# Building the token table of a mixture-of-experts layer: scatters to DRAM against matmuls of 0/1 rows

## The reference, cut to what matters

```python
expert_id = g_idx * EXPERTS_PER_GROUP + e_local        # two experts for each token, of 32
dest = pstart[e_sorted] + (jnp.arange(A) - start[e_sorted])   # a slot for each (token, choice)
x_disp = jnp.zeros((P, D), h.dtype).at[dest].set(h[t_sorted]) # blocks of rows, one expert each
def expert_block(args):
    xb, e = args
    return (jax.nn.silu(xb @ w_gate[e]) * (xb @ w_up[e])) @ w_down[e]
contrib = (w_sorted[:, None] * y_disp[dest].astype(jnp.float32))
out = jnp.zeros((T, D), jnp.float32).at[t_sorted].add(contrib)
```

## Time and profile before

| what | us |
|---|---|
| median of three runs | 3354.77 |
| lowest, highest | 3348.31, 3357.60 |
| span of the profiled execution | 3367.8 |
| PE busy in it | 2546.5 (76%) |
| DVE busy in it | 1126.7 (33%) |
| ACT busy in it | 943.4 (28%) |
| POOL busy in it | 375.3 (11%) |

### The profile page before, as it was taken

The page is one execution under the profiler, slowest core; times in us unless marked ns, Lnnn a source line. Parts: engine busy times, 40 slices in busy tenths (PEclk is TensorE's granted clock), DMA queues, the critical chain, the costliest instruction groups (busy, mean ns, idle before and its releaser), DMA issues. The chain is left out here.

```text
span 3367.8 us, 50960 instructions
## 1 busy us (share of the span) xinstructions
PE 2546.5 (76%) x17895; PEld 1960.9 (58%) x17896; DVE 1126.7 (33%) x2432; ACT 943.4 (28%) x1720; POOL 375.3 (11%) x716
## 2 busy tenths in 40 slices
PE   5974798387778759699897388884969898648773
PEld 4964698154445438576676266653847676536562
DVE  4446334210001025447443211115634653311113
ACT  2233322121112122246322033322234532113221
POOL 0000000111111110000000223221000000122222
PEclk9987899698889879799998588886979998768896
DMA  3201221699999953122121789994122123299995
GB/s 115 77 1 51 76 88 51 222 369 374 374 369 369 374 189 120 32 63 63 48 55 63 238 248 302 313 295 136 51 56 62 45 58 89 82 293 303 307 326 173
DMA packets 416210, 582.37 MB, mean 173 GB/s; under 512 B 24674, under 2 KB 299746, under 8 KB 416076
## 3 DMA queue, kind: packets, MB, share of 16 engines
q1 hardware_dynamic: 397932, 538.84, 48.7%
q0 software_dynamic: 18144, 41.74, 4.5%
HBM read 559.47 MB, written 35.97 MB: 177 GB/s over the span
## 5 line engine op out<-in xcount | busy, mean ns | idle before, releaser
L1007 PE MATMUL ps<-e_wg,e_xT 128*64 128x128 f32 (+1 forms) x2688 | 438.9, 327 | 103.1 <-issue 91.6
L1007 PEld LDWEIGHTS ps<-e_wg,e_xT 128*64 128x64 f32 x2688 | 353.8, 150 | 236.2 <-issue 189.1
L1009 PE MATMUL ps<-e_wu,e_xT 128*64 128x128 f32 (+1 forms) x2688 | 438.6, 327 | 0.0
L1147 DVE TENSOR_TENSOR e_hid<-e_silu,ps 64x128 f32<-64x128 f32 (+1 forms) x210 | 69.7, 334 | 990.9 <-ACT e_silu L1057 946.0
L1009 PEld LDWEIGHTS ps<-e_wu,e_xT 128*64 128x64 f32 x2688 | 353.3, 150 | 0.0
L1029 PE MATMUL ps<-e_wd,e_hidT 128*64 128x512 f32 x1112 | 310.2, 694 | 9.1 <-ACT e_hidT L1060 6.6
L1882 PE MATMUL ps<-t_hT,t0a_t0g_w 128*128 128x512 f32 x768 | 199.2, 411 | 4.6 <-DVE t0a_t0g_w L1904 2.3
L1882 PE MATMUL ps<-t_hT,t1a_t1g_w 128*128 128x512 f32 x768 | 199.2, 411 | 4.6 <-DVE t1a_t1g_w L1904 2.4
L1057 ACT ACTIVATE e_silu<-ps 64x128 f32<-64x128 f32 (+1 forms) x210 | 63.0, 303 | 488.3 <-PE ps L1009 487.6
L447 POOL TENSOR_TENSOR all_x<-all_x,ln_rows 128x1024 f32<-128x1024 f32 x16 | 48.2, 3040 | 1261.7 <-DVE all_x L440 1261.7
L1882 PEld LDWEIGHTS ps<-t_hT,t1a_t1g_w 128*128 128x128 f32 x768 | 145.4, 194 | 45.7 <-issue 10.3
(11 more groups left out here) (594 smaller groups left out, 4711.2 us busy)
## 6 DMA issues: line engine op xcount, KB each, us to landing
e_wd<-in_w_down SPq DMA_DIRECT2D x32, 2048.0 KB
e_wd<-in_w_exp_down SPq DMA_DIRECT2D x64, 1024.0 KB
e_wg<-in_w_exp_gate SPq DMA_DIRECT2D x54, 1024.0 KB
e_wu<-in_w_exp_up SPq DMA_DIRECT2D x54, 1024.0 KB
e_wg<-in_w_gate SPq DMA_DIRECT2D x22, 2048.0 KB
e_wu<-in_w_up SPq DMA_DIRECT2D x22, 2048.0 KB
m_h<-in_w_gate SPq DMA_DIRECT2D x10, 2048.0 KB
m_hT<-in_w_up SPq DMA_DIRECT2D x10, 2048.0 KB
```

What stands on the lines that cost most here:

```text
L1007: nc.tensor.matmul(ps_gu[q][0:SLOTS], xT[:, c, :], wg[s][:, c, span], start=c == 0, stop=c == DC - 1)
L1009: last = nc.tensor.matmul(ps_gu[q][SLOTS:P], xT[:, c, :], wu[s][:, c, span], start=c == 0, stop=c == DC - 1)
L1147: vec.tensor_tensor(hid[SLOTS:P, q], silu[SLOTS:P, q], ps_gu[q][SLOTS:P], ALU.mult).then_inc(hid_ready, 1)
```

## The change

The scatters, the filled table in DRAM, the readbacks and the transpose go. VectorE splits each slot into its block and its place in the block, by adding and taking off 12582912, at which size a float holds only whole numbers. It compares both with rows of running numbers: `at_pos` has a 1 in the place's column, `at_blk` a 1 in the block's column, which is then multiplied by the pair's number plus 1. TensorE sums the products of these over the tokens in PSUM, eight times for each of the two copies of the places, so that `ps_tok` holds the pair's number plus 1, or 0 at an empty place. The columns of integers are then made of that. SP no longer waits for the scatters, nor reads anything back.

```diff
 constants:
-            for n in ("ident", "mask_le", "mask_lt", "mask_ge", "second"):
+            for n in ("ident", "mask_le", "mask_lt", "mask_ge"):
                 g.memset(k[n][:], 0.0)
+            g.memset(k["second"][:], -2.0)
...
-            g.iota(k["choice"][:], [[S, 2], [P, TT]], 0, 1, ...).then_inc(made, 1)
+            g.iota(k["iota_pos"][:], [[1, SLOTS]], 0, 0, ...)
+            g.iota(k["iota_blk"][:], [[1, TABLE]], 0, 0, ...)
+            g.iota(k["choice"][:], [[S, 2], [P, TT]], 1, 1, ...).then_inc(made, 1)
...
 moe, SP:
-                sp.wait_ge(zero_ready, 1)
-                sp.dma_start(token_dram..., zero[:]).then_inc(zero_stored, 16)
                 sp.dma_start(rows_dram..., h_rows).then_inc(rows_stored, 16)
...
-                sp.wait_ge(token_scattered, 16 * 2 * TT)
-                for q in range(2):
-                    sp.dma_start(tokrow[:, q], token_dram...).then_inc(tokrow_landed, 16)
                 for n in range(EARLY, len(first)):
...
 moe, PE:
-                pe.wait_ge(tokrow_landed, 32)
-                nc.tensor.transpose(ps_tok, tokrow..., ident[0:nb, 0:nb]).then_inc(tokT_ready, 1)
+                pe.wait_ge(hot_slots_ready, 1)
+                for j in range(2):
+                    for t in range(TT):
+                        for q in range(2):
+                            last = nc.tensor.matmul(ps_tok[q * SLOTS:(q + 1) * SLOTS], at_pos[:, j, t, :],
+                                                    at_blk[:, j, t, :], start=j + t == 0, stop=j + t == TT)
+                last.then_inc(tokT_ready, 1)
...
 moe, DVE:
-                vec.memset(zero[:], float(2 * S)).then_inc(zero_ready, 1)
...
-                vec.tensor_copy(sloti[:], slotf[:]).then_inc(table_ready, 1)
+                link(vec.tensor_scalar(blk_up[:], slotf[:], 1.0 / SLOTS, 0.5 / SLOTS - 0.5, ALU.mult, ALU.add))
+                link(vec.tensor_scalar(blk_up[:], blk_up[:], ROUND, None, ALU.add))
+                link(vec.tensor_scalar(blk[:], blk_up[:], -ROUND, None, ALU.add))
+                link(vec.scalar_tensor_tensor(pos[:], blk[:], -float(SLOTS), slotf[:], ALU.mult, ALU.add))
+                vec.tensor_tensor(at_pos[:].rearrange("p j t s -> p (j t) s"),
+                                  k["iota_pos"][:].unsqueeze(1).to_broadcast([P, 2 * TT, SLOTS]),
+                                  pos[:].rearrange("p j t -> p (j t)").unsqueeze(2).to_broadcast([P, 2 * TT, SLOTS]),
+                                  ALU.is_equal)
+                flat = at_blk[:].rearrange("p j t b -> p (j t) b")
+                link(vec.tensor_tensor(flat, k["iota_blk"][:].unsqueeze(1).to_broadcast([P, 2 * TT, TABLE]),
+                                       blk[:].rearrange("p j t -> p (j t)").unsqueeze(2).to_broadcast([P, 2 * TT, TABLE]),
+                                       ALU.is_equal))
+                vec.tensor_tensor(flat, flat, k["choice"][:].rearrange("p j t -> p (j t)").unsqueeze(2).to_broadcast(
+                    [P, 2 * TT, TABLE]), ALU.mult).then_inc(hot_slots_ready, 1)
                 dve.wait_ge(tokT_ready, 1)
-                link(vec.tensor_scalar(part[:, 0], ps_tok, 1.0, None, ALU.mult))
-                link(vec.tensor_scalar(part[:, 1], part[:, 0], float(S), float(-S), ALU.is_ge, ALU.mult))
-                link(vec.tensor_tensor(part[:, 2], part[:, 0], part[:, 1], ALU.add))
-                vec.tensor_scalar(choicecol[:], part[:, 0], 2.0, k["second"][:], ...).then_inc(tokcol_ready, 1)
-                vec.tensor_scalar(tokcol[:], part[0:SLOTS, 2], float(S - 1), None, ALU.min).then_inc(tokcol_ready, 1)
+                vec.tensor_scalar(part[:, 0], ps_tok, 1.0, float(4 * S + 2), ALU.is_lt, ALU.mult)
+                vec.tensor_scalar(part[:, 1], ps_tok, float(S), float(-S), ALU.is_gt, ALU.mult)
+                link(vec.tensor_scalar(part[:, 2], ps_tok, 2.0, k["second"][:], ALU.mult, ALU.add))
+                link(vec.scalar_tensor_tensor(part[:, 3], ps_tok, -1.0, part[:, 1], ALU.add, ALU.add))
+                vec.tensor_tensor(choicecol[:], part[:, 2], part[:, 0], ALU.add).then_inc(tokcol_ready, 1)
+                vec.tensor_scalar(tokcol[:], part[0:SLOTS, 3], 0.0, None, ALU.max).then_inc(tokcol_ready, 1)
...
 moe, POOL:
-                pool.wait_ge(zero_stored, 16)
                 pool.wait_ge(rows_stored, 16)
-                pool.wait_ge(table_ready, 3)
-                for t in range(TT):
-                    for j in range(2):
-                        nc.gpsimd.indirect_dma_start(token_dram, ..., k["choice"][:, j, t:t + 1], None)
+                pool.wait_ge(table_ready, 2)
                 pool.wait_ge(tokcol_ready, 2)
```

More of the change, by code:

```diff
@@ L28 @@
 TABLE = MAX_BLOCKS + 2
-ROWS = TABLE * SLOTS
+ROUND = 12582912.0
 class Stage:
@@ L739, in constants @@
                          ("mask_ge", [P, 2 * S - P], F32),
-                         ("iota_e", [P, NE], F32), ("group_of", [P, NE], F32), ("choice", [P, 2, TT], F32), ("second", [P, 1], F32)):
+                         ("iota_e", [P, NE], F32), ("group_of", [P, NE], F32), ("iota_pos", [P, SLOTS], F32), ("iota_blk", [P, TABLE], F32), ("choice", [P, 2, TT], F32), ("second", [P, 1], F32)):
         k[n] = st.sb(n, shape, dt)
@@ L753, in _ @@
                    allow_small_or_imprecise_dtypes=True)
-            g.iota(k["choice"][:], [[S, 2], [P, TT]], 0, 1, allow_small_or_imprecise_dtypes=True).then_inc(made, 1)
+            g.iota(k["iota_pos"][:], [[1, SLOTS]], 0, 0, allow_small_or_imprecise_dtypes=True)
+            g.iota(k["iota_blk"][:], [[1, TABLE]], 0, 0, allow_small_or_imprecise_dtypes=True)
+            g.iota(k["choice"][:], [[S, 2], [P, TT]], 1, 1, allow_small_or_imprecise_dtypes=True).then_inc(made, 1)
             pool.wait_ge(made, 1)
-            g.affine_select(k["second"][:], k["second"][:], [[0, 1]], ALU.is_ge, 1.0, SLOTS - 1, -1)
+            g.affine_select(k["second"][:], k["second"][:], [[0, 1]], ALU.is_ge, -1.0, SLOTS - 1, -1)
             g.affine_select(k["ident"][:], k["ident"][:], [[-1, P]], ALU.not_equal, 1.0, 0, 1)
@@ L827, in moe @@
         slotf = st.sb("slotf", [P, 2, TT])
-        sloti = st.sb("sloti", [P, 2, TT], U32)
+        blk = st.sb("blk", [P, 2, TT])
+        blk_up = st.sb("blk_up", [P, 2, TT])
+        pos = st.sb("pos", [P, 2, TT])
+        at_pos = st.sb("at_pos", [P, 2, TT, SLOTS])
+        at_blk = st.sb("at_blk", [P, 2, TT, TABLE])
         table = st.sb("table", [1, 2, NE], I32)
-        zero = st.sb("zero", [TABLE, SLOTS])
-        tokrow = st.sb("tokrow", [TABLE, 2, SLOTS])
-        part = st.sb("part", [P, 3, TABLE])
+        part = st.sb("part", [P, 4, TABLE])
         tokcol = st.sb("tokcol", [SLOTS, TABLE], U32)
@@ L848, in moe @@
         rows_stored = st.sem("rows_stored")
-        zero_ready = st.sem("zero_ready")
-        zero_stored = st.sem("zero_stored")
         logits_ready = st.sem("logits_ready")
@@ L859, in moe @@
         table_ready = st.sem("table_ready")
-        token_scattered = st.sem("token_scattered")
-        tokrow_landed = st.sem("tokrow_landed")
+        hot_slots_ready = st.sem("hot_slots_ready")
         tokT_ready = st.sem("tokT_ready")
@@ L907, in _ @@
                 sp.dma_start(bias[:, NG:], b_re.partition_broadcast(P)).then_inc(router_landed, 16)
-                sp.wait_ge(zero_ready, 1)
-                sp.dma_start(token_dram.rearrange("(b s) one -> b (s one)", s=SLOTS), zero[:]).then_inc(zero_stored, 16)
                 sp.dma_start(rows_dram.rearrange("(t p) d -> p t d", p=P), h_rows).then_inc(rows_stored, 16)
@@ L913, in _ @@
                     load(s, s, m)
-                sp.wait_ge(token_scattered, 16 * 2 * TT)
-                for q in range(2):
-                    sp.dma_start(tokrow[:, q], token_dram.rearrange("(b s) one -> b (s one)", s=SLOTS)).then_inc(tokrow_landed, 16)
                 for n in range(EARLY, len(first)):
@@ L977, in _ @@
                 last.then_inc(rank_ready, 1)
-                pe.wait_ge(tokrow_landed, 32)
-                nb = TABLE
-                nc.tensor.transpose(ps_tok, tokrow[:].rearrange("b q s -> b (q s)"), ident[0:nb, 0:nb]).then_inc(tokT_ready, 1)
+                pe.wait_ge(hot_slots_ready, 1)
+                for j in range(2):
+                    for t in range(TT):
+                        for q in range(2):
+                            last = nc.tensor.matmul(ps_tok[q * SLOTS:(q + 1) * SLOTS], at_pos[:, j, t, :], at_blk[:, j, t, :],
+                                                    start=j + t == 0, stop=j + t == TT)
+                last.then_inc(tokT_ready, 1)
                 pe.wait_ge(table_ready, 2)
```

4 lines of the change are left out of this document (removed).

## The result

The changed kernel took 3337.14 us, the median of six runs, against 3357.16 for the kernel before beside it. One of the six runs, 3630.92 us, fell in a slow state of the chip (mean granted clock 0.705 where the others have 0.871 to 0.874) and is left out of the ratio: 0.9926 [0.9900, 0.9952], 25 us off (16 to 34). The bare medians differ by 20.0 us, and by 22.4 without that run. Two repeats beside later runs of the kernel before gave 0.9917 and 0.9915, 28 and 29 us by the ratio and 23.8 and 24.8 by the medians. Forecast were 35. The direction was right. The forecast counted from a kernel before of 3354.77 us; times 0.9926 that is 3329.9, inside the range of 3310 to 3333 by 3 us, while the bare median of 3337.14 is 4 us above it. The sum was 6 to 10 us too large by the ratios, and 10 to 15 by the medians.

The account below looks back on a forecast made before the run. Expert stages bound by the weight stream, with TensorE's start as second clock: 11.0 (e0) + 13.5 (e1) + 10.8 (e2) - 0.3 (constants) = 35.0 us off, 3354.8 to 3320; range 3310 to 3333.

Parts of the forecast that it names:

- The two clocks: Each expert stage: gains the stream's hole where the weight stream leads, TensorE's earlier start where the ring fills once.
- e2: Third expert stage: stream leads, gaining its hole's 9.0, SP's dropped fill 0.4 and a later stand's 1.4; 10.8 us.
- e1: Second expert stage: the ring fills, so everything moves by TensorE's shift; gain 13.5 us.
- e0: First expert stage: the stream leads, gaining its hole's 10.6 us and SP's dropped fill of 0.4; gain 11.0 us.
- Rival 1: Stream holes are worth nothing, the stream catches up, only e1 gains; 3341.6 us, chance 0.14.
- The start of TensorE: Cast of the slots to POOL's step: 6.0 us in place of 19.25, so 13.3, 13.5, 12.7 earlier in e0, e1, e2.
- The sixteen matmuls: Table product on TensorE: eight pairs at 0.21 us plus 0.2, so 1.9 us; bounds 0.9 and 3.8.
- 13.3 earlier, more than the stream's 11.0, so the stream leads to the end: e0: TensorE frees the first refill 13.3 us earlier, so it does not hold the stream; gain 11.0.
- rival 3: A stage's first gathers suffer from the unpaused stream; 20 us more would give about 3372, chance 0.03.
- I take the holes as closed: Stream holes behind the scatters: all of 10.6, 9.7 and 9.0 us regained; bound from below 80%.
- The 1.4 us for the short stand at 3025.59: e2: the stream's one later wait for TensorE loses 1.4 us and closes, as TensorE's shift of 12.7 is larger.
- a stage shorter by less than 9: Sign listed as showing the forecast wrong: any expert stage gaining less than 9 us.

Follow-up runs that it names:

- held_stream: Changed kernel, but SP holds the rest of the first ring's loads until the first gather has landed; 0.9948 against the kernel before.
- late_table: Changed kernel, with VectorE repeating the at_pos comparison 18 times so the table comes late while the stream runs free; 0.9985 against the kernel before.
- after_again: The changed kernel, unchanged, run again beside the kernel before; 27.9 us off by the ratio, 23.8 by the medians.
- late_table_half: Changed kernel, with nine repeats of the at_pos comparison on VectorE, half the delay; 0.9937 against the kernel before.
- before_again: The kernel before, unchanged, run beside itself to show the scatter; its second profile has 3359.1 us.
- deep_first_ring: Changed kernel, with five weight loads in flight instead of two while the ring first fills; 0.9888 in four runs, 0.9911 in six when repeated.
- early_spare: Changed kernel, with POOL's store of the spare row moved ahead of its wait for the finished columns; 0.9924 against the kernel before.
- scatter_free_stream: Kernel before, scatters and DRAM table kept, with the scatter wait and both readbacks moved from SP's queue to ACT's; 1.0031, slower by 10 us.
- deep_spare_held_e1: Changed kernel, with five loads in flight, the early spare store, and SP held for the first gather in e1 alone; 0.9933, 3337.27 us.

## Why the prediction was right, and where its terms were off

**The two clocks stand, and both are needed.** Beside one and the same kernel before (3361.80 us) the table alone gave 17.5 us (held_stream), the free stream alone 5.0 (late_table), both together 27.9 (after_again); by the medians it is 16.1, 4.7 and 23.8. And the free stream with the table left in DRAM cost 10. The 10 us between the first and the last of these lie at the edge of their intervals; the stages are clearer: e2 has 399.4 with the stream held and 384.8 to 392.7 in all kernels with the table from matmuls and a free stream. That e2 gains by the stream and e1 by TensorE's start is thereby shown, and that e0 needs both; what it gained with its hole kept (7.3) goes beyond the two clocks. Rival 1 (holes worth nothing) falls with late_table's e2, 10.6 us shorter by the stream alone.

**The start of TensorE: right in its sum, and by luck in the largest part.** The sixteen matmuls took the forecast 1.9. These are the summaries of this line in the changed kernel and of the rank sums in before:

```profile
L978 PE MATMUL ps<-e_at_blk,e_at_pos x96: 310/310/347, 643.2 to 2938.8; 128*64 128x50 f32 x96
L976 PE MATMUL ps<-e_both,all_ones x24: 401/401/401, 634.9 to 2954.0; 128*128 128x32 f32 x24
```

The first has 32 records a stage for sixteen matmuls, the second 8 for the four that the code issues (one for each t): an f32 matmul leaves two records. So the 0.21 us between rows is the step from one pair of records to the next, and a pair of matmuls with 128 columns moving takes two such steps. By that row eight pairs would have made 3.4 us and 0.2 to the end; the prediction counted half as many steps. What saved it is that it also left the step at 0.21: with 50 columns moving it is 0.11 us (1.95 less the last record's 0.31, over fifteen steps). The two errors cancel. Its bound from above is off in the same way: the rank sums are four matmuls in 1.90 us, so sixteen of them would be 7.6, not 3.8. The rule of the Trainium skill ("TensorE: Matmul & The Clock Gate", Back-to-back issue gap) gives 42 ns for 50 columns at the lower clock; measured are 0.11 us a step and 0.24 us for each pair of matmuls, so the trace does not agree. The 128x400 comparisons took 0.57, not 0.54. POOL's step stands 0.67 us behind the end of the last column step (646.13 + 0.17 to 646.97), not 0.3. Sum 6.4 for 6.0.

**e0: right, with the two clocks close to each other.** It gained 11.7 for 11.0. As forecast, its stream has no hole left: from 28 to 580 us into the stage no stretch of 3 us in the changed kernel has a DMA share under 0.9. (The forecast said the same of e1 and e2 up to the first full ring; there single ones, around 37 us in e1 and 55 to 58 us in e2, have 0.84 and 0.60 to 0.88.) The stream's issue is 12.3 us ahead behind the hole (the load at 641.98 is 32.2 us after the stage's start, the one at 654.61 44.5) and keeps 12 to the end. The step "13.3 earlier, more than the stream's 11.0, so the stream leads to the end" holds with a margin of about a microsecond only: in late_table_half, with a shift of 7.1, the loads are no more than that ahead for most of the stage. held_stream shows the other side: its loads were 4 to 5 us ahead, with TensorE 15.6 ahead, and e0 gained 7.3.

**e1: the shift was mis-sized.** Forecast 13.5, measured 9.3. That TensorE leads is right: SP's queue in e1 of the changed kernel still stands once for 21 us,

```profile
1940.24 0.37 SPq L903 DMA_DIRECT2D e_wd<-in_w_exp_down  x1
1961.19 0.37 SPq L903 DMA_DIRECT2D e_wg<-in_w_exp_gate  x1
```

which ends 109.25 us into the stage; the last such stand of before ended 120.64 in,

```profile
1986.61 0.38 SPq L902 DMA_DIRECT2D e_wg<-in_w_exp_gate  x1
```

so in the changed kernel it comes 11.4 earlier (11.8 in the mean of all profiles of the two kernels). But TensorE's shift was read off at POOL's step (19.52 - 6.38 = 13.1 as measured), and what counts is the first turned tile. There it is 12.2 (59.1 to 46.9). The step that failed is that the piece behind POOL's step was taken as unchanged, since the first gather "already ran beside" the stream: before, SP had resumed shortly ahead of that gather, and from its issue to the tile it took 7.2 and 6.2 us in e1; with the stream never paused it takes 8.2 to 8.4, and 5.5 with the stream held. So rival 3's mechanism is real and takes 1 to 2 us of this stage against before, not the 13 at which it would decide. Of the other 2 to 3 us it can only be said that they are lost after the tile and lie within what e1 differs from run to run (5.5 us in before, 2.8 in the changed kernel). Nor does e1 follow the tile one for one at every size: late_table_half, 5.5 us ahead at the tile, gained 0.7, and held_stream, 14.8 ahead, gained 13.9.

**e2: the hole was mis-sized, and some of it is given back.** Forecast 10.8, measured 4.2. SP's queue in e2 of the changed kernel:

```profile
2940.56 0.37 SPq L903 DMA_DIRECT2D e_wu<-in_w_exp_up  x1
```

This load, the eleventh, is 37.7 us into the stage. Before it was 45.2,

```profile
2972.60 0.39 SPq L902 DMA_DIRECT2D e_wu<-in_w_exp_up  x1
```

so it comes 7.5 us ahead, not 9.4. In before_again it was 43.7, so 6.0 ahead; over all profiles the lead here is 6.6. Part of that is that the load in front of it, the tenth, goes out 29.3 us into the stage and not 28.4: SP's dropped fill didn't bring its 0.4 us. Then the lead shrinks. From the issue of this load to that of the eighteenth it is 23.9 and 24.8 us in the two profiles of before and 25.6, 26.2 and 27.3 in the three of the changed kernel, so that 4.5 us of lead are left. It looks as if a stream that has paused came back faster, but that is not it: in late_table, whose stream never pauses either, the same loads take 20.8 us, and in late_table_half 22.4. These are the 20 us from 38 us into e2 in the changed kernel, in late_table and in deep_first_ring, columns as in the earlier trace rows:

```profile
2940.87:2960.87 20.00, 9.31 (x94) 8.00 (x94) 1.97 (x4) 0.96 (x4) 4.11 (x10) 0.66 0.98 311
2965.84:2985.84 20.00, 0.00 (x0) 0.00 (x0) 12.35 (x23) 0.00 (x0) 1.92 (x4) 0.50 1.05 351
2944.01:2964.01 20.00, 7.97 (x88) 7.22 (x90) 1.97 (x4) 0.96 (x4) 3.47 (x9) 0.66 1.07 342
```

With two loads in flight the stream moves 309 to 311 GB/s here in the three profiles of the changed kernel (322 in early_spare), in which the first blocks already run, and 347 and 351 in the two kernels whose TensorE starts later. 311 against 351 over 20 us are 20 x (1 - 311/351) = 2.3 us. With five in flight it keeps 342 to 345 beside the same blocks. So TensorE's earlier start itself takes about 2 us back from the stream, and the deeper queue gives them back; whether it is the blocks' gathers or their stores was not separated. In the lengths of the whole stage the same order shows, less clearly: 384.8 to 388.1 in the three kernels with a free stream and a later TensorE, 386.1 to 388.3 in the three with the deeper queue, 389.0 to 392.7 in the changed kernel, but 387.9 in early_spare.

The stage's last load,

```profile
3267.82 0.37 SPq L903 DMA_DIRECT2D e_wd<-in_w_exp_down  x1
```

is 365.0 us in, against 371.6 and 375.1 in the two profiles of before; the two other profiles of the changed kernel have it at 369.4 and 370.1. On average 5.2 us of lead are left there. The step that failed is "I take the holes as closed", with its bound of 80% "should the stream after it run slower": it held for the share, which is 1.06 in the hole's place, and not for the lead. That began at 6.6 us instead of 9.4, the stream after it did run slower, and 5.2, some half of the forecast, were left, where the bound had 80%. The price at 373 GB/s, the rate of e0's larger loads, was the smaller error: at the 309 GB/s that before has in e2 from 3000 to 3250 us, the same as in e1, the hole is 11 x (1 - 67/309) = 8.6 us instead of 9.0. The 1.4 us for the short stand at 3025.59 were not found.

**The constants** cost 0.26 us ahead of the first load (8.77 to 9.03), as said. Sum of the measured terms: 11.7 + 9.3 + 4.2 - 0.3 = 24.9; measured are 25 to 29 by the ratios and 20 to 25 by the medians. The range held with a share of luck: its lower end allowed e1 and e2 some 3 us each, they missed by 4.2 and 6.6, and what took that up was the room left for e0, which was not needed, and for the spread of the runs. In the forecast's list, "a stage shorter by less than 9" was named as what would be wrong, and e2 is that stage; the first gather over 10 us was not seen in the changed kernel.

## What to carry to other kernels

A wait that holds the bulk stream may be protecting the small, latency-bound transfers beside it: price its removal as the hole closed less what those transfers then cost, or first move them off memory, as this change does. With two clocks in a stage, read each one's shift where the two meet (here the first turned tile, not the end of the table), and price a hole at the rate of the stream that follows it in that same stage. And before a forecast rests on 2 or 3 us of a stage, take a second profile of the same kernel: here they differed by up to 5.5.

## What the runs showed of the hardware beyond that

- Eight scatters of 128 single numbers beside a running stream of weights: the readback could go out 9.8 us after the last was issued, against 2.8 with the stream held (both e0).
- During these scatters the DMA engines are full and move less. This stretch of scatter_free_stream has a share of 1.01 at 268 GB/s, where the full stretches of e0 had 368 to 373:

```profile
647.00:666.00 19.00, 0.00 (x0) 0.00 (x0) 0.00 (x0) 1.28 (x1) 3.22 (x4) 0.50 1.01 268
```

- The first gather of 64 rows of a stage, from issue to turned tile: 5.3 to 5.8 us with the stream held (held_stream, and e1 of deep_spare_held_e1), 7.8 to 9.4 beside it in the changed kernel, with two loads in flight. Single blocks later in e1 and e2 reach 10.5 and 11.2, in the kernel before as well.
- Loads of 1 MB, two in flight, early in e2: 309 to 311 GB/s with the first blocks beside them, 347 to 351 without; five in flight 342 to 345 with them. The DMA engines' share is 0.98 to 1.07 in all of these, so that it doesn't tell them apart.
- Sixteen matmuls of f32, 64 columns of weights, 50 moving, by halves of the array at a granted clock of 0.50 (1.2 GHz): 1.95 us, about as long as four with 128 columns of weights and 32 moving (1.90). Each f32 matmul leaves two records in the trace: 32 for the sixteen, 8 for the four.
